# Dealing the last head's output matmuls and the linear-attention fillers anew, in a four-layer float32 block on one NeuronCore

## What is computed

```python
def hybrid_layer(...):            # layers 0 and 1 of the first block
    hx, hc = modulated rms_norm of latent / context tokens
    px, pc = split_cols(hx @ w_in + b_in), split_cols(hc @ w_in + b_in)
    ya = conv_module(*p[0:3])     # 31-tap depthwise conv, layer norm, w_conv_out
    yb = gla_branch(p[3:9])       # gated linear attention, 4 heads, both directions
    yc = attn_branch(p[9:13])     # 8 query heads, 2 key/value heads, rotary, softmax
    xs = xs + gate_x * ((sigmoid(p[13])*ya + sigmoid(p[14])*yb + sigmoid(p[15])*yc) @ w_out)

def gla_scan(q, k, v, log_a, s0): # chunks of 64 tokens, state carried from chunk to chunk
    att = where(mask, q_in @ k_in.T, 0);  o = att @ v + q_in @ S_prev
    S = exp(last) * S_prev + k_state.T @ v

def second_block(...):            # two more layers: 4 mLSTM heads and 4 retention heads,
    ...                           # chunks, head layer norm, gates
        y = concatenate([y_m, y_r]) @ w_out[l];  x = x + gate * y
```

## Time and profile before

| | |
|---|---|
| median of 3 runs | 3299.59 us (3297.2 to 3299.6) |
| the profiled execution, its own time | 3300.26 us |
| its span in the profile | 3298.3 us |
| mean granted TensorE clock | 0.978 |
| PE busy | 3164.9 us, 96% |
| DVE / ACT / POOL busy | 1366.0 / 846.0 / 1539.9 us |
| share of the chain that ended last: PE | 86% |
| the same: DVE | 8% |

### The profile page before, as it was taken

The page is one execution under the profiler, slowest core; times in us unless marked ns, Lnnn a source line. Parts: engine busy times, 40 slices in busy tenths (PEclk is TensorE's granted clock), DMA queues, the critical chain, the costliest instruction groups (busy, mean ns, idle before and its releaser), DMA issues.

```text
span 3298.3 us, 40515 instructions
## 1 busy us (share of the span) xinstructions
PE 3164.9 (96%) x15123; PEld 2302.9 (70%) x15123; DVE 1366.0 (41%) x2573; ACT 846.0 (26%) x1547; POOL 1539.9 (47%) x1451
## 2 busy tenths in 40 slices
PE   7999998999999999998989999999998999999989
PEld 4666675665656555465778768888994688889955
DVE  3021346544564412226666555444332363443322
ACT  4122226421111022324411222332111123322111
POOL 1688987000000059971353325776550157775600
PEclk9999999999999999998999999999999999999999
DMA  6111110023443121110233422222221222222202
GB/s 222 52 39 32 31 35 14 14 79 125 128 138 130 41 64 39 45 39 1 68 115 116 140 66 77 72 70 77 65 77 51 66 77 77 65 77 65 76 28 75
DMA packets 259907, 236.59 MB, mean 72 GB/s; under 512 B 20950, under 2 KB 257410, under 8 KB 259716
## 3 DMA queue, kind: packets, MB, share of 16 engines
q1 hardware_dynamic: 259716, 234.02, 23.4%
HBM read 231.91 MB, written 2.10 MB: 71 GB/s over the span
## 4 chain that ended last, share of the span: by engine, by line
PE 86%; DVE 8%; POOL 2%; ACT 2%; issue 1%; SPq 1%; DMA 0%; DVEq 0%; ACTq 0%; POOLq 0%
PE ps L481 27%; PE ps L1219 23%; PE ps L526 11%; PE ps L1053 5%; PE ps L512 3%; DVE arena L1905 2%; PE ps L1277 2%; PE ps L796 2%; DVE arena L1909 1%; PE ps L1321 1%; PE ps L809 1%; ACT arena L1375 1%; PE ps L1158 1%; DVE bQz L1909 1%; DVE small L2176 1%
## 5 line engine op out<-in xcount | busy, mean ns | idle before, releaser
L2604 POOL TENSOR_TENSOR arena<-arena,posi 128x512 f32<-128x512 f32 (+1 forms) x360 | 412.3, 1145 | 30.0
L481 PE MATMUL ps<-hT,wring 128*128 128x512 f32 (+1 forms) x1184 | 406.4, 503 | 0.7 <-ACT arena L1375 0.7
L526 PE MATMUL ps<-hT,wring 128*128 128x512 f32 (+1 forms) x1024 | 376.9, 523 | 0.4 <-ACT arena L1375 0.2
L481 PEld LDWEIGHTS ps<-hT,wring 128*128 128x128 f32 x1184 | 228.3, 194 | 170.1 <-issue 155.5
L1375 ACT ACTIVATE arena<-ps 128x256 f32<-128x256 f32 (+4 forms) x395 | 171.6, 434 | 642.4 <-PE ps L481 235.2
L2686 POOL TENSOR_TENSOR arena<-wring 128x512 f32<-128x512 f32 x72 | 91.8, 1275 | 491.8 <-PE ps L1219 297.2
L526 PEld LDWEIGHTS ps<-hT,wring 128*128 128x128 f32 x1024 | 194.1, 194 | 154.0 <-issue 145.1
L481 PE MATMUL ps<-arena,wring 128*128 128x512 f32 (+1 forms) x768 | 278.7, 523 | 3.0 <-issue 3.0
L2603 POOL TENSOR_SCALAR posi<-arena,cols 128x512 f32<-128x512 f32 (+1 forms) x360 | 245.7, 683 | 35.4
L1905 DVE TENSOR_TENSOR arena<-arena 128x768 f32<-128x768 f32 (+7 forms) x120 | 171.2, 1426 | 192.8 <-ACT arena L1375 188.9
L1375 ACT ACTIVATE arena<-ps,cols 128x512 f32<-128x512 f32 (+2 forms) x172 | 100.8, 586 | 545.8 <-PE ps L481 298.6
(11 more groups left out here) (271 smaller groups left out, 5068.1 us busy)
## 6 DMA issues: line engine op xcount, KB each, us to landing
wring<-in_w_in SPq DMA_DIRECT2D x126, 1024.0 KB, 5.4
wring<-in_w_mod SPq DMA_DIRECT2D x24, 1024.0 KB, 8.6
wring<-in_w_out SPq DMA_DIRECT2D x24, 1024.0 KB, 5.8
wring<-in_w_ada SPq DMA_DIRECT2D x21, 1024.0 KB, 5.2
wring<-in_w_conv_out SPq DMA_DIRECT2D x7, 512.0 KB, 6.1
wring<-in_w_gla_out SPq DMA_DIRECT2D x7, 512.0 KB, 6.1
wring<-in_w_attn_out SPq DMA_DIRECT2D x7, 512.0 KB, 5.5
arena<-in_w_ada SPq DMA_DIRECT2D x3, 1024.0 KB, 5.2
```

The source lines that it names most:

```text
L481: last = eng.matmul(o_(out), a, b_, start=(i == 0), stop=(i == len(parts) - 1))
L526: mm = eng.matmul(bank[b][:, 0:n], w[:, k, j * P:(j + 1) * P], hT[:, k, t0:t0 + n], start=(k == 0), stop=(k == KD - 1))
L2604: pool.link(eng.tensor_tensor(dst, dst, scratch, ALU.add))
```

## The change

Four things change.

1. **Output matmuls dealt.** The 42 early output matmuls of the last head are no longer three blocks of 14 but nine shares, 3, 5, 4, 5, 4, 6, 4, 7 and 4, one after each item of the last head's core. The first waits for `ys` of head 5, and only the 13th of tile 0 for head 6. `claim(4, 5)` after them is gone.
2. **Fillers dealt.** `gla_core` takes `parts` and `lead`: `lead` pieces run before the first scores (after the `kst` transposes and `claim(7)`), the rest is dealt evenly over the 12 steps, where before it was `rate` a step until it ran out. The leads are 1, 2 for the first pair (d = 0, 1) and 0, 1 for the second. Key tiles are cut into pieces of 1024 columns.
3. **Three value blocks in attention.** Value blocks 3, 4 and 5 (`late`) run after `scores(0)` inside `attend`, on banks 4 and 6; ACT evacuates them at the start of its `attend`, ahead of the first probabilities.
4. **Queries rotated ahead.** On PE `turned("q", 2)` and `turned("q", 3)` come before `gla_spread`; on DVE the reciprocal of the query norms and `rotated` q 2 and 3 come before `gla_scaled`. POOL's `four_sums` in layer 1 waits for `gla out done` too.

```diff
+OUT_SHARES = [3, 5, 4, 5, 4, 6, 4, 7, 4]
+LATE_VALUES = 3
...
-            a = [[("out", n, j)] for j in range(OUT_EARLY)]
+            ends = np.cumsum(OUT_SHARES).tolist()
+            a = [[("out", n, e - share, e)] for e, share in zip(ends, OUT_SHARES)]
...
-            def gla_core(l, p, d, between, rate):
+            def gla_core(l, p, d, between, parts, lead):
...
                 claim(7)
                 scan = (0, 1) if d == 0 else (1, 0)
+                for _ in range(lead):
+                    next(between)
+                ends = [(parts - lead) * n // 12 for n in range(13)]
                 att(order[0])
...
-                        for _ in range(rate):
-                            next(between, None)
+                        for _ in range(ends[si + 1] - ends[si]):
+                            next(between)
...
                 for n in range(len(pairs) + 2):
                     if n < len(pairs):
                         scores(n)
+                    if n == 0:
+                        rings[0] = {"A": [4, 6], "V": []}
+                        for _ in late:
+                            pass
...
-                            project(("ak", l, g, sg), w, g * P, hT, KD, sg)
-                            yield
+                            t0, n = SEG[sg]
+                            key = ("ak", l, g, sg)
+                            b = next_bank("A", key)
+                            for k in range(KD):
+                                mm = eng.matmul(...)
+                                if k % (2 * TX // n) == 2 * TX // n - 1:
+                                    yield
...
-                gla_core(l, 0, 0, islice(filler, len(segs(l)) * 12), 2)
-                gla_core(l, 0, 1, filler, 2)
+                half_parts = len(segs(l)) * 12
+                gla_core(l, 0, 0, islice(filler, half_parts), half_parts, 1)
+                gla_core(l, 0, 1, filler, half_parts, 2)
...
-                gla_core(l, 1, 0, by_part("aq", C_AQ, 2, 2), 1)
-                gla_core(l, 1, 1, keys_values(), 1)
+                gla_core(l, 1, 0, by_part("aq", C_AQ, 2, 2), len(segs(l)) * 8, 0)
+                late = keys_values()
+                gla_core(l, 1, 1, islice(late, 12 + 6 - LATE_VALUES), 12 + 6 - LATE_VALUES, 1)
...
-                next(between, None)
-                gla_spread(l, 1)
                 turned("q", 2)
                 next(between, None)
                 turned("q", 3)
+                next(between, None)
+                gla_spread(l, 1)
...
-                        eng.wait_ge(*at(("ys", l, 6)))
-                        for k in range(14):
+                        for j, k in (divmod(i, 14) for i in range(*x)):
+                            if k == 0:
+                                claim(7 - j)
+                                w_out.append(weights(wv(I["w_out_2"][l], j * P, P), 16, P))
+                            if j == 0 and k in (0, 12):
+                                eng.wait_ge(*at(("ys", l, 6 if k else 5)))
                             eng.matmul(bank[7 - j][:, 0:TX], w_out[j][:, k, :], ys[:, k, :], start=(k == 0), stop=False)
...
-                claim(4, 5)
```

More of the change, by code:

```diff
@@ L925, in keys_values @@
                         for sg in both:
-                            project(("ak", l, g, sg), w, g * P, hT, KD, sg)
-                            yield
+                            t0, n = SEG[sg]
+                            key = ("ak", l, g, sg)
+                            b = next_bank("A", key)
+                            for k in range(KD):
+                                mm = eng.matmul(bank[b][:, 0:n], w[:, k, g * P:(g + 1) * P], hT[:, k, t0:t0 + n],
+                                                start=(k == 0), stop=(k == KD - 1))
+                                if k == KD - 1:
+                                    mm.then_inc(*pe.tell(("full", key)))
+                                if k % (2 * TX // n) == 2 * TX // n - 1:
+                                    yield
                     used(("full", ("ak", l, 1, "c")))
@@ L1018, in _ @@
                     pass
-                attend(l)
+                attend(l, late)
                 rings[0] = WIDE
@@ L1530, in attend @@
                 att_no[0] += len(pairs)
+                for u in range(6 - LATE_VALUES, 6):
+                    evac(("av", l, 0, u), av[:, u, :], 0, P)
+                m.mark(("av", l), *m.at[("free", ("av", l, 0, 5))])
                 eng.wait_ge(*at(("q inverse", l)))
@@ L1707, in _ @@
                         evac(("ak", l, g, sg), ak[:, g, t0:t0 + n], 0, n, ACT.Identity, bias=col(l, B_AK + g))
-                for u in range(6):
+                for u in range(6 - LATE_VALUES):
                     evac(("av", l, 0, u), av[:, u, :], 0, P)
-                m.mark(("av", l), *m.at[("free", ("av", l, 0, 5))])
                 between = by_job("ag", ag, B_AG, 0)
@@ L2344, in _ @@
                 rotated("q", 1)
-                gla_scaled(l, 1)
-                m.mark(("branch", l, 1), *m.at[("gla out done", l, 1)])
-                rotated("q", 2)
-                rotated("q", 3)
                 u0 = units(l)[0]
@@ L2351, in _ @@
                 rcp(qscale[:, :, u0:6, :], qscale[:, :, u0:6, :], ("q inverse", l))
+                rotated("q", 2)
+                rotated("q", 3)
+                gla_scaled(l, 1)
+                m.mark(("branch", l, 1), *m.at[("gla out done", l, 1)])
                 attend(l)
```

14 lines of the change are left out of this document (6 added, 8 removed).

## The result

The changed kernel takes 3267.69 us (median of 4 runs, 3261.16 to 3273.75) beside 3298.39 us (4 runs, 3294.52 to 3299.6) for the kernel before. The ratio is 0.9909, 95% interval 0.9881 to 0.9936: about 30 us less. The forecast was 3258 with a range of 3243 to 3273: the direction and the range held, the point lies 9.7 us too low, outside its own narrower range of 3252 to 3264.

The account below looks back on a forecast made before the run. PE bounds the kernel, so only its idle and low-clock time can be won. Gains of 27.7 + 4 + 10 = 41.7 us off 3300.3 give 3258.6, by the median 3258; own range 3252 to 3264, wider range 3243 to 3273.

Parts of the forecast that it names:

- Part 1: Last head's output matmuls: dealt shares cover each chunk's DVE and ACT latency; 15.5 us in layer 0, 12.2 in layer 1.
- the bank wait: End of the early output matmuls: PE's 1.48 us at `claim(4, 5)`, waiting for DVE to read tile 2, goes.
- Part 2: Linear attention's fillers: moving the pieces removes idle time, 2.5 us in layer 0 and 1.5 in layer 1, together 4.
- the half pace behind it stays: Layer 0's first pair, between directions: lead takes only 0.65 of the 3.89 us wait, and PE's low clock behind it remains.
- rival C: Linear attention: leads start at once and the clock holds, +19 us at most, about +15 likely, 3243 us; chance 0.12.
- Parts 3 and 4: Attention's start: late value blocks and earlier query rotations gain 2.5 us in layer 0, 7.5 in layer 1, together 10.
- What POOL takes back: Layer 1's attention: POOL's four sums start after the late blocks, beside the first two or three pairs, costing 1.7 us.
- The sum: Whole kernel: gains of 27.7, 4 and 10 us add to 41.7, taken off the profiled 3300.3 us.
- A: Attention's start gives nothing net through late probabilities, lower clock and POOL; gain 32 to 34 us, 3267 us; chance 0.20.
- B: Output matmuls: the chunk chain still shows between the shares, 5 us a layer, 3268 us; chance 0.08.
- D: Layer 1's attention: POOL keeps DVE late, PE idles at 1.2 GHz; slower than before, up to 3336 us; chance 0.03.
- E: Output shares: weights or banks 6 and 5 come late, PE waits inside; 20 us of part 1 lost, 3279; chance 0.05.

Follow-up runs that it names:

- the old deal: Changed kernel with projections dealt as before in each layer's first three cores and no leads, keys and values still dealt evenly: 3265.65 us, ratio 0.9902.
- the second edit: Changed kernel with ACT making the first probabilities before evacuating the three late value blocks, bank 5 added to their ring: alone 3266.12 us, ratio 0.9894.
- the second measurement: The changed kernel run again unaltered, against the kernel before: 3267.47 us, ratio 0.9904.

## Why the prediction was right, and where not

**Part 1** was right in mechanism and size. Forecast 27.7 us, measured 27.6 by undoing it (good to some 6 us) and 27.5 by the traces. The stretches take 51.91 and 52.01 us where I had 51.4 and 51.4 behind a wait of 1.4, and that wait (1.41) is there. Summing PE's work at full clock was enough, because every gap got more filler than the 5.3 us of DVE and ACT. My 1.48 us for the bank wait was its idle time alone; with the clock behind it, it cost up to 3.5 us in layer 0, by one trace of each kernel.

**Part 2** was right about the leads and wrong about their price. They stand behind ACT's evacuation, by 3.26 us, as counted from the banks. That "the half pace behind it stays" failed: the lead ran at full clock, and layer 0 gave 6.2 us, not 2.5. In layer 1 the traces show no gain of 1.5: linear attention is 0.6 us longer, with 37.5 us at the low clock up to the last scores, and 30.7 with the old deal. By the timed runs the whole part is worth nothing. My upper bound, that the leads start at once and the clock with them, was rival C, about 15 us. Banks of their own make it so, and this measured 15 us alone (ratio 0.9858) and 20 us with the second edit. How the 15 us divide over waits and clock is not shown: the one trace has its gain in layer 1 and none in layer 0, where the wait of 3.26 us went.

**Parts 3 and 4** came near their size in the traces (7.7 us of 10), and the timed runs do not confirm it: undoing part 4 cost nothing, and undoing part 3 cost 4.6 us within overlapping intervals. The reason given for layer 1 was half right: moving the rotations does free them of POOL, but the late blocks do it too, since they hold POOL's sums back. What POOL takes back was sized at 1.7 us, in a form that I had argued away. I wrote that the lock "hardly" speaks against the new place, since most DVE work there reads PSUM. But the one small operation that does not, 0.16 us long, takes 2.36 us beside POOL. The page "SBUF — State Buffer" of the Trainium skill, section "SBUF: two separate sides", says that a DVE instruction with two SBUF inputs is blocked for the whole of a GpSimd instruction that came first. The trace agrees: the operation starts at 1508.82 us, 0.03 behind POOL's sum of 2.37 us, and ends 0.02 behind it. I had applied the rule by the bulk of the bytes instead of by the chain. For the table load the trace has 1.28 us and the first exponential right behind it (243.00 after 241.71). The page "ScalarE: Activation LUTs" of the Trainium skill, section "What ACT_TABLE_LOAD costs", has 2.66 us with a drain; here the measurement decides.

**The sum** is the step that failed. The stretches that I costed gained 40.8 us where I had 41.7, and the kernel gained 30. I took every other stretch as fixed, and it is not. Here are windows of 250 us over layer 1's recurrence, before and then changed, with four short ones inside each. They stand at the same four places of the work, where PE comes from small matmuls with 4 rows to the scores of a chunk; at the last three it also waits 1.1 to 1.4 us for ACT. The last columns are clock, DMA share and GB/s.

```profile
2691.00:2694.50 3.50, 3.50 (x22) 2.64 (x22) 0.38 (x2) 3.04 (x7) 2.55 (x2) 1.00 0.98 298
2766.00:2769.50 3.50, 3.13 (x10) 2.78 (x11) 0.96 (x4) 3.41 (x5) 2.14 (x1) 0.56 0.80 275
2842.00:2845.50 3.50, 3.50 (x13) 3.12 (x14) 0.37 (x2) 3.05 (x4) 2.59 (x2) 0.58 0.60 208
2916.00:2919.50 3.50, 2.64 (x15) 2.43 (x16) 1.26 (x4) 3.35 (x4) 1.64 (x1) 1.00 0.90 294
2685.00:2935.00 250.00, 246.38 (x1340) 218.79 (x1340) 99.85 (x259) 81.65 (x138) 183.81 (x155) 0.99 0.23 71
```

```profile
2664.00:2667.50 3.50, 3.50 (x10) 2.76 (x10) 1.87 (x6) 1.41 (x4) 3.27 (x4) 0.55 0.18 59
2739.00:2742.50 3.50, 3.50 (x10) 2.85 (x10) 0.29 (x1) 2.39 (x3) 3.26 (x2) 0.53 0.46 161
2814.00:2817.50 3.50, 3.50 (x11) 2.87 (x10) 0.29 (x1) 2.55 (x4) 3.09 (x2) 0.52 0.53 182
2889.00:2892.50 3.50, 3.50 (x13) 2.90 (x12) 0.36 (x2) 2.74 (x4) 2.90 (x2) 0.51 0.58 203
2655.00:2905.00 250.00, 246.76 (x1324) 218.25 (x1323) 98.42 (x257) 81.11 (x137) 180.27 (x153) 0.97 0.22 68
```

The clock falls to 1.2 GHz (about 0.5) at two of the four places before, and at all four after, in the same work. The second trace of each kernel has it again at two (the second and the fourth) and at all four. Here is the fourth place in the first trace of the kernel before, in its second, and in the changed kernel:

```profile
2916.86 0.71 PE L481 MATMUL ps<-arena 128*128 128x128 f32 x4 [1.11 <-ACT arena L1375]
...
2917.63 1.89 PE L1219 MATMUL ps<-hT,wring 128*128 128x256 f32 x8
```

```profile
2913.41 0.71 PE L481 MATMUL ps<-arena 128*128 128x128 f32 x4 [1.09 <-ACT arena L1375]
...
2914.18 3.19 PE L1219 MATMUL ps<-hT,wring 128*128 128x256 f32 x8
```

```profile
2888.53 0.78 PE L484 MATMUL ps<-arena 128*128 128x128 f32 x4 [1.08 <-ACT arena L1395]
...
2889.53 3.34 PE L1240 MATMUL ps<-hT,wring 128*128 128x256 f32 x8
```

The wait is the same, and the eight recorded instructions behind it take 1.89 us at full clock and 3.19 or 3.34 us where it fell. Layer 1's recurrence took 532.5 us in both traces of before, and 533.9 to 537.3 in all twelve traces of the changed kernel and its variants. PE's idle time in it is no longer than before (6.2 us in the changed kernel, 6.5 and 6.4 before), but the time at the low clock is 13.7 us instead of 6.8, and half of that difference, 3.4 us, covers the 3.2 us of the table. With layer 0's, the two recurrences took 1062.4 and 1065.7 us before and 1067.9 to 1071.4 in the twelve. So some 4 to 5 us of a gain made elsewhere are given back there, to the clock and not to a wait; with two traces of before the size is rough. Why the changed kernel meets more low clock in this stretch is not shown: no experiment shifted the work alone.

Another 6 us lie between the traces (37.0) and the timed runs (30.7 by the medians, 31.6 by the ratio of the second measurement). One kernel's executions spread over 12 us (3261.2 to 3273.8, at clocks of 0.984 to 0.980) and those of the kernel before on one chip over 16 us (3291.7 to 3308.1, at clocks of 0.981 to 0.976). A difference of clock times the span, 0.004 and 0.005 of some 3280 us, is 13 and 16 us by estimate, so the clock alone can account for the spread. The two traces of the changed kernel, 3260.0 and 3263.6 us, lie below the middle of its nine executions. So two traces are a small sample, and I leave this part open.

**The rivals.** The measured time is that of A (3267), but A's mechanism is not shown: in the traces attention's start gives 7.7 us, and the timed runs above are too coarse to tell 7.7 from nothing. B, D and E are excluded by the trace: there is no chunk wait, attention in layer 1 has a clock of 1.00 from 1525 to 1575 us, and the shares run without waits. None of the signs of being wrong that the prediction names came: the leads did not run straight behind the transposes, and the clock of attention's first 30 us is 0.89.

## What to carry to other kernels

When filler is put ahead of a wait, look at which buffer the filler itself needs: here leads and deal together were worth nothing measurable while the leads shared banks with the operand that was late, and once that operand had banks of its own the leads were worth 15 us. Deal filler over the gaps of a chain, a little more than each gap's latency in each, and sum the engine's work at full clock to know what can be won. Where a clock falls behind short waits or small matmuls, a sum over the changed stretches alone is too good: here the untouched ones took back some 4 to 5 us of 41, so keep that for the forecast, and time an edit of a few us by repeated runs, not by a trace. The further version (key halves on banks 2 and 3, first probabilities ahead of the late blocks) takes 3249.2 us, ratio 0.9843 to the kernel before, the fastest of all that ran.

## What the runs showed of the hardware

- A VectorE operation on 128x1 with two inputs from SBUF took 0.16 us, and 2.36 us beside a GpSimd sum of 2.37 us, as if it had been as long as its neighbour.
- A TensorE wait of 1.1 us can cost more than twice that: where the granted clock fell behind it, eight recorded matmul instructions took 3.34 instead of 1.89 us. The same wait in the same code was followed by the low clock in one trace of one kernel and not in its other trace. At the first of the four places the clock fell in the changed kernel with no wait at all, behind small matmuls with 4 rows, and it did not fall there in the kernel before.
- A TensorE wait of 3.26 us, followed by projections, was followed by full clock in layer 0 (eight instructions in 3.67 us). A wait of 2.35 us in layer 1, with another of 2.21 us just ahead of it, was followed by the same eight in 6.06 us.
- Executions of one unchanged kernel differ by 12 to 16 us with the mean granted clock (0.981 to 0.976 for the kernel before), and every profiled pair of kernels must be read against that.
